# The prompt's attention items: the first two begun beside Q's last tiles, and long and short items alternated

## The reference

```python
def diff_attend(q, q_pos, segments, lam):
    ...
        s = jnp.einsum('bqhmd,bkhmd->bhmqk', q, k).astype(jnp.float32) * scale
        visible = (k_pos[None, :] // CHUNK) <= (q_pos[:, None] // CHUNK)
        scores.append(jnp.where(visible, s, -1e30))
    p = jax.nn.softmax(jnp.concatenate(scores, axis=-1), axis=-1)
    p = p[:, :, 0] - lam * p[:, :, 1]
    ...
        out = out + jnp.einsum('bhqk,bkhe->bqhe', p[..., start:start + n].astype(v.dtype), v)
```

## Time and profile before

| | us |
|---|---|
| median of 3 runs (2562.28 to 2566.25) | 2565.28 |
| profiled execution, its own time | 2566.88 |
| its span in the profile | 2565.1 |
| TensorE busy, share of the span | 2395.5, 93% |
| VectorE, ScalarE, GpSimd busy | 1572.5, 1139.2, 639.7 |

### The profile page before, as it was taken

One profiled execution on the slowest core, in us unless ns is written; L12 is line 12 of the kernel. 1 busy time (PEld: TensorE's weight loads), 2 busy tenths in 40 slices (PEclk: granted clock), 3 DMA queues, 4 the chain that ended last, 5 costly groups with the idle time before them and its releaser, 6 DMA issues. The chain is left out here.

```text
span 2565.1 us, 41962 instructions
## 1 busy us (share of the span) xinstructions
PE 2395.5 (93%) x16903; PEld 2301.7 (90%) x16903; DVE 1572.5 (61%) x2270; ACT 1139.2 (44%) x1845; POOL 639.7 (25%) x619
## 2 busy tenths in 40 slices
PE   7999999998988979999999999997898889999996
PEld 7989998998987979999999999997665689999996
DVE  4988769557796566446745565447454577555444
ACT  3345633545524545335644453336443445444332
POOL 3257401215011244112111132122111244122112
PEclk9999999999988989999999999998588899999998
DMA  8567664454753535454566655443202145665451
GB/s 217 154 188 218 194 201 153 130 166 135 231 160 99 166 117 146 145 151 144 158 207 197 180 163 153 147 146 114 66 1 74 50 132 173 181 181 157 146 151 61
DMA packets 699699, 381.65 MB, mean 149 GB/s; under 512 B 24713, under 2 KB 688754, under 8 KB 699506
## 3 DMA queue, kind: packets, MB, share of 16 engines
q1 hardware_dynamic: 666288, 337.16, 45.2%
q10 hardware_dynamic: 33218, 41.81, 5.0%
HBM read 361.29 MB, written 17.63 MB: 148 GB/s over the span
## 5 line engine op out<-in xcount | busy, mean ns | idle before, releaser
L426 PE MATMUL tile_ps<-xh,wh 128*128 128x320 f32 (+1 forms) x3584 | 1088.8, 304 | 59.5 <-POOL xl L659 35.7
L410 DVE TENSOR_TENSOR wl<-raw,wh 128x1024 fp32r<-128x1024 f32 (+1 forms) x640 | 788.9, 1233 | 568.4 <-ACT wh L404 566.9
L427 PE MATMUL tile_ps<-xl,wh 128*128 128x320 f32 (+1 forms) x3584 | 1073.1, 299 | 0.0
L428 PE MATMUL tile_ps<-xh,wl 128*128 128x320 f32 (+1 forms) x3584 | 1072.5, 299 | 0.0
L404 ACT CAST wh<-raw 128x1024 fp32r<-128x1024 f32 (+1 forms) x640 | 655.0, 1025 | 764.1 <-PE tile_ps L428 750.9
L426 PEld LDWEIGHTS tile_ps<-xh,wh 128*128 128x128 f32 x3584 | 691.6, 193 | 72.4 <-DVE wl L410 29.1
L427 PEld LDWEIGHTS tile_ps<-xl,wh 128*128 128x128 f32 x3584 | 693.1, 193 | 1.2 <-issue 0.4
L428 PEld LDWEIGHTS tile_ps<-xh,wl 128*128 128x128 f32 x3584 | 692.4, 193 | 0.0
L520 POOL TENSOR_TENSOR hl<-hf,hh 128x256 fp32r<-128x256 f32 (+1 forms) x176 | 250.9, 1425 | 1247.1 <-ACT hh L462 1247.0
L426 PE MATMUL tile_ps<-hh,wh 128*128 128x256 f32 (+1 forms) x1408 | 423.5, 301 | 22.9 <-POOL hl L520 11.3
L427 PE MATMUL tile_ps<-hl,wh 128*128 128x256 f32 (+1 forms) x1408 | 417.4, 296 | 0.0
(11 more groups left out here) (252 smaller groups left out, 1921.7 us busy)
## 6 DMA issues: line engine op xcount, KB each, us to landing
raw<-in_ffn_w_in_dram SPq DMA_DIRECT2D x352, 512.0 KB, 3.7
raw<-in_ffn_w_out_dram SPq DMA_DIRECT2D x128, 448.0 KB, 3.5
raw<-in_ffn_w_out_dram SPq DMA_DIRECT2D x64, 512.0 KB, 3.7
raw<-in_ssm_w_glu_dram SPq DMA_DIRECT2D x32, 512.0 KB, 3.8
raw<-in_attn_w_kv_dram SPq DMA_DIRECT2D x32, 512.0 KB, 3.9
wt<-scr_w ACTq DMA_DIRECT2D x16, 512.0 KB, 4.3
cp<-scr_c ACTq DMA_DIRECT2D x16, 512.0 KB, 3.4
raw<-in_attn_w_q_dram SPq DMA_DIRECT2D x16, 512.0 KB, 3.7
```

The source lines that it names most:

```text
L410: nc.vector.tensor_tensor(wl[n % WS][:, 0:k, :], raw[n % RAWS][:, 0:k, :], wh[n % WS][:, 0:k, :].bitcast(F32), ALU.subtract).then_inc(w_lo, 1)
L426: nc.tensor.matmul(o, wh[w][:, kk, :], xa, start=kk == 0, stop=False)
L427: nc.tensor.matmul(o, wh[w][:, kk, :], xb, start=False, stop=False)
L428: mm = nc.tensor.matmul(o, wl[w][:, kk, :], xa, start=False, stop=kk == ROWS[n] - 1)
```

## The change

Three things change. The order of the items becomes head by head: first every head with block 3 and then block 0 (four key tiles, one key tile), then every head with block 2 and then block 1 (three, two). The first two items begin inside the stage ("q", 1): their scores stand behind tiles 4 and 5 (counted from 0) on TensorE, their maxima behind tiles 4 and 5 on VectorE, the combine of item 0 behind tile 6, their exponentials behind tiles 5 and 6 on ScalarE. These two items' scores go to `misc` (banks 0 and 1, banks 2 and 3) instead of `tile_ps`, which Q's tiles use. And `ex`, `pT`, `qs`, `qd` and others lie in other places, in the parts of `xh` and `xl` that the first half used, so that they can be written while the second half's Q tiles are read. GpSimd clears and fills `qs` from the start of ("q", 1).

```diff
-        xm2 = Map(x_at)
-        ex = [xm2(f"ex{s}", [P, 2, SEQ]) for s in range(2)]
-        pT = [xm2(f"pT{s}", [P, SEQ]) for s in range(2)]
-        qs = [xm2(f"qs{s}", [P, 2, P]) for s in range(2)]
-        exS = [xm2(f"exS{s}", [P, PAST + DEC]) for s in range(2)]
-        kTc = [xm2(f"kTc{s}", [P, PAST]) for s in range(2)]
-        qd = [xm2(f"qd{s}", [P, P]) for s in range(2)]
-        sqb = xm2("sqb", [P, D])
-        assert xm2.at <= x_end
-        xm3 = Map(x_at)
-        pTS = [xm3(f"pTS{s}", [P, (PAST // P + 1) * P]) for s in range(2)]
+
+        xa = Map(x_at)
+        ex = [xa(f"ex{s}", [P, 2, SEQ]) for s in range(2)]
+        xa = Map(xl_at)
+        qd = [xa(f"qd{s}", [P, P]) for s in range(2)]
+        pts_at = xa.at
+        pT = [xa(f"pT{s}", [P, SEQ]) for s in range(2)]
+        qs = [xa(f"qs{s}", [P, 2, P]) for s in range(2)]
+        assert xa.at <= xl_at + 4 * DT * NT[0]
+        exS, kTc = [], []
+        for s in range(2):
+            xb = Map((x_at, xl_at)[s] + 4 * DT * NT[0])
+            exS.append(xb(f"exS{s}", [P, PAST + DEC]))
+            kTc.append(xb(f"kTc{s}", [P, PAST]))
+            assert xb.at <= (xl_at, x_end)[s]
+        pTS = [Map((x_at, pts_at)[s])(f"pTS{s}", [P, (PAST // P + 1) * P]) for s in range(2)]
...
-        def item(i, j, k):
-
-            it = 2 * j + 8 * i + k
-            return it // NH, it % NH, k % 2, it
-
-        def at_end(i, j, k):
-            return 8 * i + 2 * j + k >= ITEMS
-
-        def prompt_pairs(body):
-
-            for i in range(4):
-                for j in range(NH // 2):
-                    body(i, j)
+
+        ITEM = [(i, h) for pair in ((3, 0), (2, 1)) for h in range(NH) for i in pair]
+
+        def item(it):
+            i, h = ITEM[it]
+            return i, h, it % 2, it
+
+        def bank_pair(it):
+
+            return misc[:, 2 * it:2 * it + 2] if it < 2 else psb[:, it % 2]
...
-            pool.wait_ge(tile_done, FIRST["o", 0])
+            pool.wait_ge(tile_done, FIRST["q", 1])
             for b in range(2):
                 G.memset(qs[b][:].rearrange("p a b -> p (a b)"), 0.0).then_inc(s_zq, 1)
                 G.memset(qd[b][:, :], 0.0).then_inc(s_zq, 1)
             pool.wait_ge(s_zq, 4)
+            for it in range(ITEMS):
+                i, h, b, _ = item(it)
+                pool.wait_ge(s_rope, (3 if i >= 2 else 2) * NH + h + 1)
+                wait(pool, s_sc, it - 1)
+                for m in range(2):
+                    G.tensor_copy(qs[b][64 * m:64 * m + 64, m, :],
+                                  head(qT, h, slice(i * P, i * P + P))[64 * m:64 * m + 64]).then_inc(s_qs, 1)
             pool.wait_ge(s_rope, 4 * NH)
-
-            def body(i, j):
-                for k in range(2):
-                    _, h, b, it = item(i, j, k)
-                    wait(pool, s_sc, it - 1)
-                    for m in range(2):
-                        G.tensor_copy(qs[b][64 * m:64 * m + 64, m, :],
-                                      head(qT, h, slice(i * P, i * P + P))[64 * m:64 * m + 64]).then_inc(s_qs, 1)
-            prompt_pairs(body)
 
             def square(i, n):
...
+        def pe_scores(pe, it):
+            i, h, b, _ = item(it)
+            mask_q, mask_k = maskrow[0:1, 0:P], maskrow[0:1, P:P + CHUNK]
+            if it == 0:
+                pe.wait_ge(s_kc, 5)
+                pe.wait_ge(s_vc, 5)
+            pe.wait_ge(s_qs, 2 * it + 2)
+            if 2 <= it < 4:
+                for n in range(FIRST["o", 0] - PSS + 2 * b, FIRST["o", 0] - PSS + 2 * b + 2):
+                    pe.wait_ge(drained[n % PSS], n // PSS + 1)
+            wait(pe, s_exp, 2 * it - 2)
+            kn = (i + 1) * P
+            for m in range(2):
+                o = bank_pair(it)[:, m]
+                nc.tensor.matmul(o[:, 0:kn], qs[b][:, m, :], head(kT, h, slice(0, kn)), start=True, stop=False)
+                mm = nc.tensor.matmul(o[:, kn - CHUNK:kn], mask_q, mask_k, start=False, stop=True)
+            mm.then_inc(s_sc, 1)
+
+
+
+        def pe_attn_start(pe):
+            yield from idle(4)
+            for it in range(2):
+                pe_scores(pe, it)
+                yield
+
+        def dve_attn_start(dve):
+            yield from idle(4)
+            for it in range(2):
+                dve_maxima(dve, it)
+                yield
+            dve_combine(dve, 0)
+            yield
+
+        def act_attn_start(act):
+            yield from idle(5)
+            for it in range(2):
+                act_exps(act, it)
+                yield
+
...
+                if it < 2:
+                    pe.wait_ge(s_exp, 4)
...
-            def body(i, j):
-                for k in range(2):
-                    transposes(*item(i, j, k))
-                    if not at_end(i, j, k + 2):
-                        scores(*item(i, j, k + 2))
-                    output(*item(i, j, k))
-            for k in range(2):
-                scores(*item(0, 0, k))
-            prompt_pairs(body)
-
+            for it in range(ITEMS):
+                transposes(*item(it))
+                if it + 2 < ITEMS:
+                    pe_scores(pe, it + 2)
+                output(*item(it))
...
+            for it in range(ITEMS):
+                i, h, b, _ = item(it)
+                act.wait_ge(s_pt, it + 1)
+                wait(act, s_o, it - 1)
+                A.copy(pT[b][:, 0:(i + 1) * P], misc[:, b, 0:(i + 1) * P]).then_inc(s_ptc, 1)
+                act.wait_ge(s_o, it + 1)
+                A.activation(otok[:, i, h * P:(h + 1) * P], misc[:, 2 + b, 0:P], ACT.Copy,
+                             scale=sts[:, b, 6:7]).then_inc(s_oe, 1)
+                if it + 2 < ITEMS:
+                    act_exps(act, it + 2)
...
-            pe_plain(pe, ("q", 1), 1, NH, X_LN3)
+            beside = pe_attn_start(pe)
+            pe_plain(pe, ("q", 1), 1, NH, X_LN3, beside)
+            finish(beside)
```

More of the change, by code:

```diff
@@ L290, in build @@
         otok = Map(h_at)("otok", [P, 5, D])
-        xm2 = Map(x_at)
-        ex = [xm2(f"ex{s}", [P, 2, SEQ]) for s in range(2)]
-        pT = [xm2(f"pT{s}", [P, SEQ]) for s in range(2)]
-        qs = [xm2(f"qs{s}", [P, 2, P]) for s in range(2)]
-        exS = [xm2(f"exS{s}", [P, PAST + DEC]) for s in range(2)]
-        kTc = [xm2(f"kTc{s}", [P, PAST]) for s in range(2)]
-        qd = [xm2(f"qd{s}", [P, P]) for s in range(2)]
-        sqb = xm2("sqb", [P, D])
-        assert xm2.at <= x_end
-        xm3 = Map(x_at)
-        pTS = [xm3(f"pTS{s}", [P, (PAST // P + 1) * P]) for s in range(2)]
+        xa = Map(x_at)
[13 more added lines that the diff above has]
+        pTS = [Map((x_at, pts_at)[s])(f"pTS{s}", [P, (PAST // P + 1) * P]) for s in range(2)]
         otx = Map(ln_at)
         obuf = [otx(f"obuf{s}", [P, T]) for s in range(2)]
+        sqb = otx("sqb", [P, D])
         assert otx.at <= ln_end
@@ L1629, in pool_attn @@
                     pool.wait_ge(s_sq, h - 1)
-        def pe_attn(pe):
[L1632 to L1644, removed]
+        def pe_scores(pe, it):
[32 more added lines that the diff above has]
+                yield
+        def pe_attn(pe):
             def transposes(i, h, b, it):
@@ L1733, in pe_attn, with dve_maxima, dve_combine @@
                 mm.then_inc(s_ot, 1)
+        def dve_maxima(dve, it):
+            V = nc.vector
+            i, _, b, _ = item(it)
+            st = sts[:, b]
+            dve.wait_ge(s_sc, it + 1)
+            V.reduce_max(st[:, 0:2], bank_pair(it)[:, :, 0:(i + 1) * P], axis=AX.X).then_inc(v_mx, 1)
+            dve.wait_ge(v_mx, it + 1)
+            V.tensor_scalar(st[:, 2:4], st[:, 0:2], -SCALE, None, ALU.mult).then_inc(s_max, 1)
+        def dve_combine(dve, it):
+            V = nc.vector
+            i, _, b, _ = item(it)
+            st = sts[:, b]
+            kn = (i + 1) * P
+            dve.wait_ge(s_exp, 2 * it + 2)
+            V.reciprocal(st[:, 6:8], st[:, 4:6]).then_inc(v_rc, 1)
+            dve.wait_ge(v_rc, 2 * it + 1)
+            V.scalar_tensor_tensor(out=st[:, 8:9], in0=st[:, 4:5], scalar=small[:, 1:2], in1=st[:, 7:8],
+                                   op0=ALU.mult, op1=ALU.mult).then_inc(v_rc, 1)
+            dve.wait_ge(v_rc, 2 * it + 2)
+            V.scalar_tensor_tensor(out=ex[b][:, 0, 0:kn], in0=ex[b][:, 1, 0:kn], scalar=st[:, 8:9],
+                                   in1=ex[b][:, 0, 0:kn], op0=ALU.mult, op1=ALU.add).then_inc(s_pr, 1)
@@ L1735, in dve_attn @@
         def dve_attn(dve):
             V = nc.vector
[L1738 to L1766, removed]
+            for it in range(ITEMS):
+                if it + 1 < ITEMS:
+                    dve_combine(dve, it + 1)
+                if it + 2 < ITEMS:
+                    dve_maxima(dve, it + 2)
@@ L1850, in build, with act_exps @@
         v_rc = sem("v_reciprocals")
+        def act_exps(act, it):
+            i, _, b, _ = item(it)
+            kn = (i + 1) * P
+            act.wait_ge(s_max, it + 1)
+            wait(act, s_pt, it - 1)
+            for m in range(2):
```

(18 more changed lines are left out.)

## The result

| | before | changed |
|---|---|---|
| median, us | 2565.13 (7 runs, 2562.28 to 2566.78) | 2573.09 (7 runs, 2567.26 to 2575.42) |
| ratio | | 1.003, 95% interval 1.0018 to 1.0041 |
| profiled execution, span | 2566.88, 2565.1 | 2575.42, 2573.6 |

The forecast was 2556.5, in a range of 2546 to 2563.5. The kernel is 8 us slower in the median; the slower side had been given a chance of 0.07. One execution of the kernel before, beside the first set of experiments, took 7327.19 us at a granted clock of 0.31, and no ratio has it.

What follows compares the result with a forecast made beforehand. TensorE was taken to bound the items, its clock deciding: -24 us at full clock (hand-over 5.1, items 109.2 against 128.2) plus 14.8 for four low pairs gave -9.2, hence 2556.5 us, range 2546 to 2563.5.

Steps and rivals of the forecast that it cites:

- the slower side: Rival: once fallen, the clock isn't granted again while one-tile items are mixed in; 2571 to 2610 us; chance 0.07.
- what bounds: Prompt attention's items: TensorE alone bounds them, at 1.2 GHz for the first half and 2.4 GHz for the second.
- the hand-over: Q's end to the first T: 7.1 us instead of 12.2, counting 4.17 of woven scores and 2.9 of waiting.
- The 5.1 us: Gain forecast for the hand-over from Q to the items; 3.7 if the table load also drained.
- the alternation's waits: Four-and-one pairs at 2.4 GHz: TensorE waits 1.4 us a pair, 0.7 for `pT` and 0.7 for `ex`.
- I take four pairs, from the first eight: Clock term: four of 16 pairs, all four-and-one, run at 1.2 GHz at 3.7 us more each, +14.8 us.
- the prediction's own formula: Items take 109.2 us at full clock, plus 3.7 per low four-and-one pair and 4.9 per low three-and-two pair.
- from seven or eight low pairs on: Number of pairs at 1.2 GHz from which the forecast had the change slower; that rival's chance was 0.07.

Runs made afterwards that it cites:

- Long items first: Changed kernel with the items in blocks 3, 2, 1, 0 (four-tile items first, one-tile last), no alternation: 2539.87 us, ratio 0.989 to the kernel before.
- the filled waits: Changed kernel with 30 unused 256-column products on TensorE at the two waits of each pair, from the third item on: 2547.35 us, ratio 0.992 to the kernel before.
- the early start alone: Changed kernel with the old order of items (blocks 0, 1, 2, 3) put back: 2560.45 us, ratio 0.9973 to the kernel before.
- the halves exchanged: Changed kernel with pairs of three and two tiles first, then pairs of four and one: 2560.2 us, ratio 0.9966 to the kernel before.
- all three kernels with long items first and the early start: Changed kernel in blocks 3, 2, 1, 0: without products 2539.87 us; with unused products in one-tile items, 128 columns 2541.52, 256 columns 2535.09.
- both kernels with the early start and the old order: Changed kernel in blocks 0 to 3: without products 2560.45 us; with an unused 256-column product in one- and two-tile items 2555.88.
- the one with blocks in its second half: Changed kernel with four-and-one pairs kept, then 8 three-tile items and 8 two-tile items in blocks: 2560.1 us, ratio 0.9969 to the kernel before.

## Why the prediction was wrong

**Right: what bounds.** TensorE bounds all the items, and its level decides. Long items first (-27 us in the medians) and the filled waits (-20) show it from two sides.

**Right: the hand-over.** 2.93 us from Q's last matmul to the first T against 2.9 worked out, and 2.62 of it waiting for `ex`. The 5.1 us were 9.4 - 5.6 = 3.8, because Q's second half took 1.4 us more beside the scores. It ran at a mean clock of 0.85 instead of 0.87, which by the same sum as above is 3 us more at 1.2 GHz and accounts for that. With the early start alone it is 6.0 us, where some 7 was expected for short items. By the Trainium skill, page "ScalarE: Activation LUTs", section "What ACT_TABLE_LOAD costs", which adds a drain of about 1380 ns to the load, T would by my estimate have come 1.4 us later. This trace doesn't agree: it shows a load of 1.28 with no gap at either side.

**Right: the alternation's waits.** Two a pair, 0.60 and 0.60 on the profile against 0.7 and 0.7, in the forecast places; 7.54 against 7.47 for a pair at full clock, and none at 1.2 GHz.

**Wrong: "I take four pairs, from the first eight".** This is the term of the sum that failed. 80 us at 1.2 GHz, at 11.2 a pair by the sum, are 7.2 pairs. With them, 5.3 in the first half and 1.9 in the second by the trace, the prediction's own formula gives 109.2 + 5.3 x 3.7 + 1.9 x 4.9 = 138.1 for the items, and 138.8 was measured: the other terms for the items, taken together, stood. For the whole change the formula then gives -24 + 28.9 = +4.9, and +6.2 with the 1.3 us that the hand-over fell short; the medians differ by 8.0. At 7.2 pairs the text had the change slower ("from seven or eight low pairs on"), and it gave that 0.07.

Two readings led to it. The first: from the old order's return of the level among three-tile items I concluded that a four-tile item in each pair would bring it back within a pair or two, and that half of the first eight pairs would run high. The level did come back after 14 us, twice, but kept only for 13.6 and 6.8 us among four-and-one pairs, and the third time it took 51. With the waits of these pairs filled it never fell. It was five low pairs of eight, and not four. The second: I put none of the low pairs into the second half. The half inherited the low level, and needed 20 us more to leave it. The kernel with three-tile items in a row in that place is 13 us faster, and with the halves exchanged the items take 12.5 us less. That part was a question of what level the work starts with, and I had treated the two halves as independent.

The old order had both ingredients apart: short items ran low anyhow, once, and long ones high, in one piece. The alternation spread the short items' effect over long ones, whose steps lose the most at 1.2 GHz (a four-tile item 7.9 instead of 4.2 us).

**What stays open.** What decides when the level falls and when it comes back. Among pairs of three and two a low stretch went on for 20 us in the second half of the changed kernel, on both profiles, and for 17 us or not at all in the first half of the exchanged one; they came into it with different levels, but more isn't shown. Why the order and the start together cost more than the two apart is open too, and whether products in the last short items pay.

## What to carry to other kernels

Where TensorE's level differs along a stretch of items, list for each order of the work what it would do at either level, and treat the level that one stretch hands to the next as a result of that order. What paid in this kernel was to put long, dense items behind the bubble and keep them together, with the short ones last; weaving the shortest between the longest to "even out" other engines cost time, since TensorE is the bound. Judge TensorE by matmuls done a microsecond, or by the granted clock, and not by its busy share, and when waits seem to cost the level, fill them once with unused products to see what the level is worth.

## What the runs showed of the hardware

TensorE was busy for 51.20 of 51.20 us and stayed at 1.2 GHz for all of it, while the kernel with 60 more matmuls in 112.5 us stayed at 2.4. Among four-and-one pairs without products the level fell in every profile taken, at the latest after 23.1 us of them. Among pairs of three and two, once it was up, it held to their end or into the last item; in one profile that was 54 us.

The length of the bubble behind Q doesn't say by itself whether the level is kept. A bubble of 2.4 us kept it when four-tile items followed (all three kernels with long items first and the early start), and one of 2.0 lost it when one-tile items followed (both kernels with the early start and the old order). With pairs of three and two behind a bubble of 2.26, one profile lost the level and one kept it. With pairs of four and one behind 2.9 us, three profiles lost it (the changed kernel twice, and the one with blocks in its second half), and the one with the waits filled, which has the same matmuls up to there, kept it. The same kernel's items took 138.8 and 138.7 us in two executions whose low stretches lay differently.
